# Folding 1/rms out of the two matmul units that follow each RMS norm

## The chip, the cores and the metric

The kernel runs on one core of a Trainium2 chip. The metric is the device time of one execution in microseconds (us), as the median of several runs. Everything is float32; the products are split in high and low parts ("hi" and "lo") so that three fp32r matmuls stand for one fp32 product.

## The reference

Two blocks of two layers each, sequence 512, width 1024, feed-forward width 2816. A layer of the first block has three RMS norms with a learned scale and shift ("adaLN"), a layer of the second block has two plain ones:

```python
def rms_norm(x, g):
    y = x * lax.rsqrt(jnp.mean(x * x, axis=-1, keepdims=True) + EPS)
    return y * g

def adaln_pre(h, g, shift, scale):
    return rms_norm(h, g) * (1 + scale) + shift

# first block, each of 2 layers; mod comes from (silu(c) @ ada_w[l] + ada_b[l])
h = adaln_pre(x, norm_g[l, 0], ...)
x = x + 0.5 * gate0 * swiglu(h, ffn1_w13[l], ffn1_w2[l])
h = adaln_pre(x, norm_g[l, 1], ...)
y = four mixers of (h @ w_in[l] + b_in[l])
x = x + gate1 * (y @ w_out[l])
h = adaln_pre(x, norm_g[l, 2], ...)
x = x + 0.5 * gate2 * swiglu(h, ffn2_w13[l], ffn2_w2[l])
# second block, each of 2 layers
h = h + mixers2(rmsnorm(h, attn_norm[l]) @ w_in[l]) @ w_out[l]
h = h + conv_ffn(rmsnorm(h, ffn_norm[l]), w_up[l], conv_w[l], conv_b[l], w_down[l])
# at the end
return rmsnorm(h, final_norm)
```

## The kernel before, in words

**Layout.** x is kept transposed in SBUF as `xT`, 8 tiles of 128 channels by 512 positions. A norm writes the tiles `hH[k]` (rounded to fp32r) and `hL[k]` (the rest), k from 0 to 7. A "unit" is one block of weights, 8 tiles of 128x128 (11 for the feed-forward's second matrix), which gives one 128x512 output in a PSUM bank: for each k the matmuls wH.hH, wL.hH and wH.hL, so 24 (or 33) matmuls a unit. In the whole program there are 508 units and TensorE (PE) does them in one fixed order.

**Engines.** Every engine has its own hand-written program and they meet on semaphores alone. For unit u:
- SyncE (SP) loads the weights into `wR[u % 2]` (`unit`, L926). It waits until the low part of unit u-2 is made.
- ScalarE (ACT) makes the high part `wH` (`hi`, L1021), after the load has landed and unit u-2 has been used by PE (semaphore `w_used`).
- VectorE (DVE) makes the low part `wL` (`lo`, L1476).
- PE multiplies (`products`, L2472) and DVE or ACT evicts the bank.

The third unit after a norm has buffers of its own (`third`, L1028, L1470), so that it can be made ready while the first two are still in use.

**Between two matmul stages** the order is: PE ends the last unit; DVE adds its output to x (`add_to_x`, L1517, in `down` or `project_out`); ACT squares the last tile of x (`last_square`, L1088); GpSimd (POOL) has by then squared and summed tiles 0 to 6 (`square_sum`, L2333, which takes two instructions a tile); PE sums both over the channels with two fp32 products by ones (`mean_square`, L2550); ACT takes Ln and Exp (`inverse_root`, L1096) and has `rstd`; then the norm proper (DVE `norm`, L1570, and ACT `norm`, L1070) for each k: DVE `hf` = x * modA * rstd, ACT `hH` = hf + shift, DVE `hL` = hf + shift - hH. `hf` has two buffers. PE begins the first two units with `first_two` (L2484), which for each k does both units' three matmuls as soon as `hL[k]` is there (semaphore `h_lo`).

**Adaptive weights.** While the feed-forward's up stage runs, SP also loads the columns of `ada_w` (`stream_ada`, L938). The first two pairs of them go to SBUF that the norm uses, so SP waits for the last `h_lo` of the norm first; four loads of 512 KB are issued then, and the load of the stage's fifth unit (index 4) stands behind them on SP's queue:

```python
turn(1, 1, False)                                   # units 2 and 3
sp.wait_ge(S.h_lo, at(S.h_lo, KT * (norm + 1)))     # L954
tiles(0, 0, False)
tiles(1, 1, False)
with sp.Fori(1, turns // 2) as i:                   # unit 4 and on
```

**Boundaries.** There are eleven norms: the first (at the start of the program), nine between two matmul stages, and the final one. The nine are: from the first feed-forward's down stage to the mixers (2), from the mixers' output projection to the second feed-forward's up stage (2), from that one's down stage to the next layer's up stage (1), from a down stage to the second block's mixers (2), and from the second block's output projection to its up stage with a convolution (2, `up2`, L2273, L3039). The first five have a shift, the last four have none.

**Mixers.** The mixers of both blocks are run in small steps between quarters of the units (`mixers_in`, L1897 for DVE and L2759 for PE). In the first block, the first unit's output goes on through a chain of small operations of DVE and ACT (steps "gates", "decay"), and PE needs their result at the end of the fourth unit (`d_running`).

## Time and profile before

| | |
|---|---|
| runs | 3773.61 us median of 3 (3773.47 to 3783.66) |
| the profiled execution | 3782.82 us, of which the span of the core is 3781.0 us |
| granted TensorE clock, mean | 0.955 of full speed |
| PE busy | 3545.8 us, 94% of the span |
| DVE busy | 1971.7 us, 52% |
| ACT busy | 1126.3 us, 30% |
| POOL busy | 333.9 us, 9% |
| DMA | 102 GB/s over the span |

The profiled execution is 9.2 us above the median of the runs. Shares of busy time are averages over all stages; PE's busy time is modelled from pipelined matmuls. In the timelines a row gives the start, the duration, the engine, the source line, the output and the inputs, how many instructions are merged, and in brackets how long the engine was idle before and what released it.

### The profile page before, as it was taken

What the parts mean: (1) busy time and instruction counts of PE and PEld (TensorE: products, weight loads), DVE (VectorE), ACT (ScalarE), POOL (GpSimd) and SP (SyncE); (2) the same over time, 40 slices, a digit from 0 to 9 for tenths busy, and PEclk for the clock granted to TensorE, in tenths of its full rate; (3) what the DMA queues carried; (4) which work ended last, traced back from release to release, by engine and by line L of the source; (5) the groups of instructions that cost most, each with busy time, mean ns of one, the idle gap of its engine ahead of it and who ended that gap; (6) DMA issues with size and microseconds to landing.
All of it is one profiled execution on the core that took longest, in us unless ns stands there. A gap on an engine that the chain in (4) does not pass through costs nothing. (4 is left out here: it accounts for less than half of the span.)

```text
span 3781.0 us, 45308 instructions
## 1 busy us (share of the span) xinstructions
PE 3545.8 (94%) x16234; PEld 2837.9 (75%) x16234; DVE 1971.7 (52%) x3061; ACT 1126.3 (30%) x1612; POOL 333.9 (9%) x271
## 2 busy tenths in 40 slices
PE   4999998998999999999898899999899999989998
PEld 2888766786888788877677778886678887668887
DVE  6563445553653366434555366435746633656643
ACT  1222333422222222223343132213433323333321
POOL 2000100131000100010013100010110001110001
PEclk7999999997999999999998899999999999999999
DMA  6553222101543255322210045321122232122232
GB/s 253 198 190 111 84 67 79 51 1 45 183 178 101 83 199 189 125 88 67 78 54 9 28 166 191 109 99 62 62 67 96 93 106 83 56 74 83 94 108 76
DMA packets 99362, 386.25 MB, mean 102 GB/s; under 512 B 10974, under 2 KB 12126, under 8 KB 98872
## 3 DMA queue, kind: packets, MB, share of 16 engines
q1 hardware_dynamic: 99256, 384.82, 29.3%
q8 instruction: 68, 1.11, 0.1%
q14 instruction: 38, 0.31, 0.0%
HBM read 382.65 MB, written 2.12 MB: 102 GB/s over the span
## 5 line engine op out<-in xcount | busy, mean ns | idle before, releaser
L1026 ACT ACTIVATE wH<-wR 128x1024 fp32r<-128x1024 f32 (+1 forms) x494 | 554.3, 1122 | 1834.3 <-PE bank L2481 1475.0
L1479 DVE TENSOR_TENSOR wL<-wR,wH 128x1024 fp32r<-128x1024 f32 (+1 forms) x494 | 652.6, 1321 | 793.6 <-ACT wH L1026 793.6
L2479 PE MATMUL bank<-hH,wH 128*128 128x512 f32 x2128 | 827.8, 389 | 0.0
L2480 PE MATMUL bank<-hH,wL 128*128 128x512 f32 x2128 | 827.8, 389 | 0.0
L2481 PE MATMUL bank<-hL,wH 128*128 128x512 f32 x2128 | 827.8, 389 | 0.0
L2479 PEld LDWEIGHTS bank<-hH,wH 128*128 128x128 f32 x2128 | 399.5, 188 | 83.0
L2481 PEld LDWEIGHTS bank<-hL,wH 128*128 128x128 f32 x2128 | 399.5, 188 | 82.8
L2480 PEld LDWEIGHTS bank<-hH,wL 128*128 128x128 f32 x2128 | 399.5, 188 | 82.7
L2479 PE MATMUL bank<-gH,wH 128*128 128x512 f32 x1056 | 410.8, 389 | 0.0
L2480 PE MATMUL bank<-gH,wL 128*128 128x512 f32 x1056 | 410.8, 389 | 0.0
L2481 PE MATMUL bank<-gL,wH 128*128 128x512 f32 x1056 | 410.8, 389 | 0.0
L2560 PE MATMUL bank<-hH,wH 128*128 128x512 f32 x704 | 307.3, 437 | 9.9 <-DVE wL L1479 9.9
L2562 PE MATMUL bank<-hL,wH 128*128 128x512 f32 x704 | 283.4, 403 | 0.0
L2561 PE MATMUL bank<-hH,wL 128*128 128x512 f32 x704 | 282.7, 402 | 0.0
L2481 PEld LDWEIGHTS bank<-gL,wH 128*128 128x128 f32 x1056 | 198.2, 188 | 41.2
L2480 PEld LDWEIGHTS bank<-gH,wL 128*128 128x128 f32 x1056 | 198.2, 188 | 41.1
L2479 PEld LDWEIGHTS bank<-gH,wH 128*128 128x128 f32 x1056 | 198.2, 188 | 41.0
L1497 DVE TENSOR_TENSOR gf<-bank,sil 128x512 f32<-128x512 f32 x88 | 60.9, 692 | 272.2 <-PE bank L2481 258.1
L2279 DVE SCALAR_TENSOR_TENSOR xn<-bank,par,xn 128x511 f32<-128x511 f32 (+1 forms) x176 | 131.6, 748 | 134.3 <-ACT xn L1388 122.4
L2560 PEld LDWEIGHTS bank<-hH,wH 128*128 128x128 f32 x704 | 137.6, 196 | 59.0 <-issue 21.5
L1438 DVE CUSTOM_DVE_ANT_0 adaw<-adaw,cond 128x1024 f32<-128x1024 f32 x144 | 170.3, 1221 | 0.0
L2340 POOL TENSOR_TENSOR sumsq<-xT 128x512 f32<-128x512 f32 x11 | 11.5, 1042 | 1752.8 <-DVE xT L1517 1732.9
(383 smaller groups left out, 4065.5 us busy)
## 6 DMA issues: line engine op xcount, KB each, us to landing
wR<-in_ffn_w SPq DMA_DIRECT2D x176, 512.0 KB, 3.4
adaw<-in_ada_w SPq DMA_DIRECT2D x144, 512.0 KB, 4.0
wR<-in_ffn_w SPq DMA_DIRECT2D x64, 704.0 KB, 4.0
wR<-in_w_up SPq DMA_DIRECT2D x88, 512.0 KB, 3.2
wR<-in_w_mix SPq DMA_DIRECT2D x76, 512.0 KB, 3.3
wR<-in_w_down SPq DMA_DIRECT2D x32, 704.0 KB, 4.1
wR<-in_w_in SPq DMA_DIRECT2D x40, 512.0 KB, 3.2
wR<-in_w_out SPq DMA_DIRECT2D x32, 512.0 KB, 3.2
```

The costliest lines, as they stand in the source:

```text
L1026: act.activation(wH[n][:, 0:tiles, :], wR[n][:, 0:tiles, :], ACT.Copy).then_inc(S.w_hi, 1)
L1438: return dve.tensor_tensor_reduce(w, w, cond[:, :], 1.0, 0.0, ALU.mult, ALU.add, dst)
L1479: dve.tensor_tensor(wL[n][:, 0:tiles, :], wR[n][:, 0:tiles, :], wH[n][:, 0:tiles, :].bitcast(F32), ALU.subtract).then_inc(S.w_lo, 1)
L1497: dve.tensor_tensor(gf[:, :], bank[1][:, :], sil[:, :], ALU.mult).then_inc(S.g_mul, 1)
L2279: dve.scalar_tensor_tensor(y, bank[half][:, 0:T - d], par[:, bass.ds(E_CW + 3 * (i + FT * half) + 2 - d, 1)], y, ALU.mult, ALU.add).then_i ...
L2340: pool.tensor_tensor(dst[:, :], xT[:, m, :], xT[:, m, :], ALU.mult).then_inc(S.pool, 1)
L2479: pe.matmul(o, wH[n][:, k, :], rH[:, r, :], start=start and k == 0, stop=False)
L2480: pe.matmul(o, wL[n][:, k, :], rH[:, r, :], start=False, stop=False)
L2481: mm = pe.matmul(o, wH[n][:, k, :], rL[:, r, :], start=False, stop=stop and k == tiles - 1)
L2560: pe.matmul(o, wH[n][:, k, :], hH[:, k, :], start=k == 0, stop=False)
L2561: pe.matmul(o, wL[n][:, k, :], hH[:, k, :], start=False, stop=False)
L2562: mm = pe.matmul(o, wH[n][:, k, :], hL[:, k, :], start=False, stop=k == KT - 1)
```

## The change

1. After each of the nine norms between stages, the first two units are no longer multiplied by the normalised h. ACT and DVE make, tile by tile in the stage before, the high and low parts of x * modA (`u_hi`, `u_lo`), and PE multiplies these (`pair`) into banks 4 and 5. Their eviction multiplies by `rstd`, and adds, where the norm has a shift, the constant (shift . W), which DVE sums from the raw weights in 16 instructions of 128x128 (`shift_sums`) and PE reduces with two products by one column of ones.
2. The mean square's two products move into that run, behind the matmuls of k = 1.
3. From the third unit on the products still use h. Its tiles are made in `norm` as before, but the scaled x of the odd tiles now comes from POOL, in two instructions (x * rstd, then * modA), and the third unit's matmuls wait for `h_lo` tile by tile. This holds for the norm at the start too, which keeps `first_two`.
4. So that the weights of those first two units are ready at the boundary, the last unit of the stage before gets buffers of its own (`last`, or `third`), and `hi_next` and `lo_next` make both units' parts while it runs. The table load for Ln and Exp moves to the start of the down stage.

On every engine the loops over the layers of both blocks become one, the `par` loads move ahead of the stage that they followed, and in the output projection DVE adds to x before it makes the next unit's low part. The core of the diff:

```diff
@@ DVE
+            def u_lo(to, hi, sub, ubase, k):
+
+                dve.wait_ge(S.u_hi, at(S.u_hi, ubase + k + 1))
+                dve.scalar_tensor_tensor(to[:, k, :], xT[:, k, :], modA[:, bass.ds(sub * KT + k, 1)],
+                                         hi[:, k, :].bitcast(F32), ALU.mult, ALU.subtract).then_inc(S.u_lo, 1)
+
+            def shift_sums(u, sub, n):
+
+                for b in range(2):
+                    dve.wait_ge(S.w_in[b], at(S.w_in[b], 16 * (u // 2 + 1)))
+                    o = gf[:, b * P:(b + 1) * P]
+                    for k in range(KT):
+                        m = mod[:, 3 * sub * KT + k:3 * sub * KT + k + 1]
+                        c = 2 * KT * n + KT * b + k
+                        if k:
+                            dve.wait_ge(S.shift, at(S.shift, c))
+                            dve.scalar_tensor_tensor(o, wR[b][:, k, :], m, o, ALU.mult, ALU.add).then_inc(S.shift, 1)
+                        else:
+                            dve.tensor_scalar(o, wR[b][:, k, :], m, None, ALU.mult).then_inc(S.shift, 1)
...
+            def project_out(ubase, sub, follow, base, shift=None):
+
+                for j in range(KT):
+                    dve.wait_ge(S.w_used, at(S.w_used, ubase + j + 1))
+                    add_to_x(j, j % 2, sub)
+                    if 1 <= j < KT - 3:
+                        lo(ubase + j + 2, KT, j % 2)
+                    elif j == KT - 3:
+                        lo_last(ubase + KT - 1, third, KT)
+                    elif j == KT - 2:
+                        if shift is not None:
+                            shift_sums(ubase + KT, follow, shift)
+                        lo_next(ubase + KT)
+                    u_lo(uL, uH, follow, base, j)
...
                 for k in range(KT):
-                    if k >= 2:
-                        dve.wait_ge(S.h_lo, at(S.h_lo, KT * n + k - 1))
-                    dve.scalar_tensor_tensor(hf[:, k % 2, :], xT[:, k, :], modA[:, sub * KT + k:sub * KT + k + 1], rstd[:, :],
-                                             ALU.mult, ALU.mult).then_inc(S.hf, 1)
+                    if k % 2 == 0:
+                        if k:
+                            dve.wait_ge(S.h_lo, at(S.h_lo, KT * n + k - 1))
+                        dve.scalar_tensor_tensor(hf[:, 0, :], xT[:, k, :], modA[:, sub * KT + k:sub * KT + k + 1], rstd[:, :],
+                                                 ALU.mult, ALU.mult).then_inc(S.hf, 1)
                     if k:
                         low(k - 1)
...
+                if not start:
+                    lo(u + 3, KT, 1)
                 low(KT - 1)
@@ POOL
+            def norm(n, sub, first=False):
...
+                pool.wait_ge(S.rstd, at(S.rstd, n + 1))
+                for k in range(1, KT, 2):
+                    if k > 1:
+                        pool.wait_ge(S.h_lo, at(S.h_lo, KT * n + k - 1))
+                    pool.tensor_tensor(hf[:, 1, :], xT[:, k, :], rstd[:, :], ALU.mult).then_inc(S.hf_x, 1)
+                    pool.wait_ge(S.hf_x, at(S.hf_x, KT // 2 * n + k // 2 + 1))
+                    pool.tensor_scalar(hf[:, 1, :], hf[:, 1, :], modA[:, sub * KT + k:sub * KT + k + 1], None,
+                                       ALU.mult).then_inc(S.hf_p, 1)
@@ PE
+            def pair(u, moving, n, ubase, shifts=None):
+
+                xH, xL = moving
+                pe.wait_ge(S.w_lo, at(S.w_lo, u + 2))
                 for k in range(KT):
+                    pe.wait_ge(S.u_lo, at(S.u_lo, ubase + k + 1))
+                    for b in range(2):
+                        o = bank[4 + b][:, :]
+                        pe.matmul(o, wH[b][:, k, :], xH[:, k, :], start=k == 0, stop=False)
+                        pe.matmul(o, wL[b][:, k, :], xH[:, k, :], start=False, stop=False)
+                        mm = pe.matmul(o, wH[b][:, k, :], xL[:, k, :], start=False, stop=k == KT - 1)
...
+                    if k == 1:
+                        if shifts is not None:
+                            pe.wait_ge(S.shift, at(S.shift, 2 * KT * (shifts + 1)))
+                            for b in range(2):
+                                mm = pe.matmul(bank[7][:, b:b + 1], gf[:, b * P:(b + 1) * P], ones[:, 0:1], start=True, stop=True)
+                            mm.then_inc(S.shift_ps, 1)
+                        mean_square(n)
+
+            def products_third(o, ready=None):
+
+                for k in range(KT):
+                    if ready is not None:
+                        pe.wait_ge(S.h_lo, at(S.h_lo, ready + k + 1))
                     pe.matmul(o, third[0][:, k, :], hH[:, k, :], start=k == 0, stop=False)
@@ ACT
+            def hi_next(u):
+
+                hi(u, u // 2 + 1, KT, 0)
+                hi(u + 1, u // 2 + 1, KT, 1, behind=3)
+
+            def u_hi(to, sub, xbase, k):
+
+                act.wait_ge(S.x_new, at(S.x_new, xbase + k + 1))
+                act.activation(to[:, k, :], xT[:, k, :], ACT.Identity,
+                               scale=modA[:, bass.ds(sub * KT + k, 1)]).then_inc(S.u_hi, 1)
@@ DVE, up: the pair's eviction, after norm
+                    if pair is not None and not later(i):
+                        dve.wait_ge(S.shift_ps, at(S.shift_ps, shifts + 1))
+                        dve.tensor_copy(cc[:, :], bank[7][:, 0:2]).then_inc(S.pair, 1)
+                        dve.wait_ge(S.w_used, at(S.w_used, ubase + 2))
+                        dve.tensor_tensor(sil[:, :], bank[4][:, :], rstd[:, :], ALU.mult).then_inc(S.pair, 1)
+                        dve.tensor_tensor(gf[:, :], bank[5][:, :], rstd[:, :], ALU.mult).then_inc(S.pair, 1)
+                        dve.wait_ge(S.pair, at(S.pair, pair + 3))
+                        dve.wait_ge(S.sil, at(S.sil, gbase + 1))
+                        dve.scalar_tensor_tensor(gf[:, :], gf[:, :], cc[:, 1:2], sil[:, :], ALU.add, ALU.mult).then_inc(S.g_mul, 1)
```

## Rows read from the trace of the kernel before

**Rows 1.** The waits of PE: engine, tile, line, releaser, us in total, times, longest.

```profile
PE bank L2490 <- DVE hL L1574: 34.7, 9, 3.9
PE bank L2555 <- ACT sqt L1092: 25.8, 10, 3.4
```

**Rows 2.** Windows around one boundary: us, busy by engine (count), clock, DMA share, GB/s.

```profile
937.20:946.90 9.70, 3.21 (x5) 0.80 (x5) 5.43 (x8) 6.62 (x8) 0.19 (x1) 0.65 0.16 54
946.90:950.40 3.50, 3.47 (x8) 2.82 (x9) 3.43 (x6) 1.45 (x2) 0.00 (x0) 0.50 0.00 0
950.40:970.80 20.40, 20.30 (x89) 16.44 (x88) 12.36 (x19) 7.39 (x9) 0.00 (x0) 1.00 0.61 218
```

**Rows 3.** Timeline of that boundary, from the output projection to the up stage.

```profile
936.82 0.39 PE L2481 MATMUL bank<-hL,wH 128*128 128x512 f32 x1
...
939.53 0.75 DVE L1517 SCALAR_TENSOR_TENSOR xT<-bank,gate,xT 128x512 f32<-128x512 f32 x1
...
943.11 0.69 ACT L1098 ACTIVATE rstd<-bank,cst 128x512 f32<-128x512 f32 x1 [1.22 <-PE bank L2555]
...
944.49 1.41 DVE L1582 SCALAR_TENSOR_TENSOR hf<-xT,modA,rstd 128x512 f32<-128x512 f32 x2 [1.28 <-ACT rstd L1101]
...
946.93 0.77 PE L2490 MATMUL bank<-hH,wH 128*128 128x512 f32 x1 [3.86 <-DVE hL L1574]
...
954.74 1.63 DVE L1574 SCALAR_TENSOR_TENSOR hL<-hf,mod,hH 128x512 fp32r<-128x512 f32 x2
...
970.82 0.39 PE L2479 MATMUL bank<-hH,wH 128*128 128x512 f32 x1
```

**Rows 4.** The same boundary: SP's queue, and ACT waiting for the fifth unit's load.

```profile
956.39 1.75 SPq L946 DMA_DIRECT2D adaw<-in_ada_w  x4
...
965.72 1.06 ACT L1026 ACTIVATE wH<-wR 128x1024 fp32r<-128x1024 f32 x1 [4.85 <-DMA wR<-in_ffn_w]
...
ACT wH L1026 <- DMA wR<-in_ffn_w: 15.6, 3, 5.4
```

**Rows 5.** Groups by line and shape: busy us, mean ns of one, idle before.

```profile
L2343 POOL TENSOR_TENSOR sumsq<-sumsq,rstd 128x512 f32<-128x512 f32 x66 | 85.5, 1295 | 5.2
...
L2340 POOL TENSOR_TENSOR sumsq<-xT 128x512 f32<-128x512 f32 x11 | 11.5, 1042 | 1752.8 <-DVE xT L1517 1732.9 <-DVE xT L1435 19.9
...
L1574 DVE SCALAR_TENSOR_TENSOR hL<-hf,mod,hH 128x512 fp32r<-128x512 f32 x80 | 59.8, 748 | 2.6
...
L1479 DVE TENSOR_TENSOR wL<-wR,wH 128x1024 fp32r<-128x1024 f32 x398 | 496.5, 1248 | 332.0 <-ACT wH L1026 332.0
...
L2167 DVE SCALAR_TENSOR_TENSOR AD<-LG,RT 128x128 f32<-128x128 f32 x8 | 2.8, 353 | 0.3
...
L1080 ACT ACTIVATE hH<-hf,mod 128x512 fp32r<-128x512 f32 x80 | 57.3, 724 | 70.3 <-DVE hf L1582 70.3
```

**Rows 6.** Timeline where POOL and DVE both read SBUF.

```profile
543.36 1.04 POOL L2356 TENSOR_TENSOR hf<-pm 128x512 f32<-128x512 f32 x1 [82.13 <-DVE pm L1902]
...
543.68 1.80 DVE L1479 TENSOR_TENSOR wL<-wR,wH 128x1024 fp32r<-128x1024 f32 x1 [0.40 <-ACT wH L1026]
...
26.27 10.78 POOL L2340 TENSOR_TENSOR rstd<-xT 128x512 f32<-128x512 f32 x1
```

**Rows 7.** Timeline of PE: an fp32 product between fp32r matmuls at full clock.

```profile
557.51 1.02 PE L2589 MATMUL bank<-hf,cst 128*128 128x512 f32 x2
...
558.60 0.40 PE L2561 MATMUL bank<-hH,wL 128*128 128x512 f32 x1
```

**Rows 8.** Timeline of PE: unit 4 after the boundaries to mixers and to up2.

```profile
437.69 0.39 PE L2481 MATMUL bank<-gL,wH 128*128 128x512 f32 x1
...
474.13 0.50 PE L2560 MATMUL bank<-hH,wH 128*128 128x512 f32 x1
...
2786.93 0.39 PE L2481 MATMUL bank<-hL,wH 128*128 128x512 f32 x1
...
2822.66 0.39 PE L2479 MATMUL bank<-hH,wH 128*128 128x512 f32 x1
```

More of the change, by code:

```diff
@@ L32 @@
 L = 2
+N_LAYERS = 2 * L
 FF = 2816
@@ L755, in build @@
         S.h_lo = sem("h_lo")
+        S.hf_x = sem("hf_x")
+        S.hf_p = sem("hf_p")
+        S.u_hi = sem("u_hi")
+        S.u_lo = sem("u_lo")
+        S.u_used = sem("u_used")
+        S.shift = sem("shift")
+        S.shift_ps = sem("shift_ps")
+        S.pair = sem("pair")
         S.mixc_in0 = sem("mixc_in0")
@@ L1518, in add_to_x, with down, tile @@
                                          xT[:, m, :], ALU.mult, ALU.add).then_inc(S.x_new, 1)
[L1520 to L1527 removed]
+            def down(ubase, sub, follow, base, between=None, shift=None):
+                def tile(m, b):
+                    for n in range(2):
+                        lo(ubase + 2 * m + 2 + n, KH, n)
                     dve.wait_ge(S.w_used, at(S.w_used, ubase + 2 * m + 2))
                     add_to_x(m, b, sub)
+                    if follow is not None:
+                        u_lo(hL, hH, follow, base, m)
                 for j in range(2 if between else 0):
                     for n in range(2):
[L1532 removed]
+                        tile(2 * j + n, 2 + n)
                         between(2 * j + n)
@@ L1570, in norm @@
-            def norm(n, sub, u=2, start=False):
+                        tile(2 * j + n, 2 + n)
+                u = ubase + 2 * KT
+                lo(u - 2, KH, 0)
+                lo_last(u - 1, last, KH)
+                dve.wait_ge(S.w_used, at(S.w_used, u - 2))
+                add_to_x(KT - 2, 2, sub)
+                if follow is not None:
+                    u_lo(hL, hH, follow, base, KT - 2)
+                    if shift is not None:
+                        shift_sums(u, follow, shift)
+                    lo_next(u)
@@ L1572, in low, with norm @@
+            def norm(n, sub, u, start=False):
                 def low(k):
@@ L1588, in norm @@
                             lo(b, KT, b)
+                if not start:
+                    lo(u + 3, KT, 1)
                 low(KT - 1)
@@ L2411, in layer1 @@
                 square_sum(KT, 2)
-            for l in range(L):
-                begin(l)
-                layer1(l)
+                norm(2, 2)
             def y_square(h):
@@ L2439, in layer2 @@
                 square_sum(0, 1)
-            for l in range(L):
-                begin(L + l)
-                layer2(l)
+                norm(1, 1)
+            for l in range(N_LAYERS):
+                begin(l)
+                if l < L:
+                    layer1(l)
+                else:
+                    layer2(l - L)
             begin(2 * L)
@@ L2512, in turn @@
                     pe.wait_ge(S.w_lo, at(S.w_lo, ubase + 2 * i + 2))
-                    pe.wait_ge(S.g_mul, at(S.g_mul, gbase + i))
+                    if not tiles or not third:
+                        pe.wait_ge(S.g_mul, at(S.g_mul, gbase + i))
                     products(bank[1][:, :], 1, KT, hH, hL, 0, True, True)
-                first_two(ubase, ready)
+                if tiles:
+                    pair(ubase, tiles, n, xbase, shifts)
+                else:
+                    mean_square(n)
+                    first_two(ubase, (S.h_lo, KT * n))
                 turn(1, True)
```

507 lines of the change are left out of this document (291 added, 216 removed).

## The prediction

> **What bounds the kernel now.** First the table: PE is busy for 94% of the span, so the time is the length of PE's queue plus its waits, and anything that makes PE wait longer at a boundary is added one for one. Second, PE's waits: between the stages it waits for the norm's tiles (9 waits, up to 3.9 us) and for the last tile's square (10, up to 3.4), 60.5 us in all [rows 1]. Third, one boundary of the mixers-to-up kind. Its last matmul ends at 936.82 + 0.39 = 937.21, which I call T0; the sum for x comes at 939.53, rstd begins at 943.11, the norm at 944.49, and PE's first product of the up stage at 946.93, 9.7 us after T0 [rows 3]. The windows add the clock: in those 9.7 us PE does 3.21 us of work, then it runs 8 matmuls in 3.5 us at a granted 0.50 (1.2 GHz), 0.43 us each, then 89 in 20.4 us, 0.229 each, at 1.00 (2.4 GHz) [rows 2]. The cold start costs 8 x 0.20 = 1.7 us. The prize is the idle 6.5 us plus this 1.7, at nine boundaries: about 70 us, if PE found work until h is ready and h came no later.
>
> My measure for every boundary is the start of the fifth unit (index 4), because units 0 to 3 are the ones that change. It is T0 + 33.6 here (970.82) [rows 3], T0 + 36.05 before the mixers and T0 + 35.3 before up2 [rows 8]. Two things precede it: the end of h, called H (954.74 + 1.63 = 956.37, so 11.9 after the norm began) [rows 3], and a load. SP waits for the last h_lo, issues four ada_w loads at 956.39, and only then unit 4's load, which ACT gets at 965.72; with the high part (1.06) and the low part (1.25) [rows 4, 5] and its handoffs unit 4 can't start before H + 11.8. ACT waits for that load 15.6 us in three stages already [rows 4].
>
> **Removed: the wait before the pair.** PE goes into x * modA at once. rstd is then found inside: 12 matmuls of 0.229 = 2.75, the shift's two products, and two fp32 products. One of these took 558.60 - 557.51 - 0.23 = 0.86 [rows 7]. The shift's products have one column and no row here; an estimate from four weight loads is 0.8 (bounds: 0 and, as full products, 1.7). 2.75 + 0.8 + 1.72 + 0.05 = 5.3, plus 1.4 from the product's end to the norm's start (943.11 to 944.49 is 1.38) [rows 3]: the norm starts at R = T0 + 6.7, or 5.9 where there is no shift. Before it was 7.3. The norm starts hardly earlier, and PE has 11 us of pair and then needs h tile by tile.
>
> **Moved: hf of the odd tiles, to POOL.** This decides the sum. POOL's two-input operation on 128x512 takes 1.295 us; for the second one, with one input and a scalar, the nearest row is the square at 1.042 [rows 5]. I take 1.04; bounds 0.52 (half of it) and 1.295. A round makes two tiles, and each round's POOL work waits for the h_lo of the last one's odd tile, since POOL has one buffer, so it is a closed loop: POOL 1.29 + 1.04, ACT's hH 0.72, DVE's hL 0.75 [rows 5], and 0.35 of handoffs (0.08 on POOL, 0.14, 0.10, 0.03) = 4.15. The DVE pipeline of before made two tiles in 11.9 / 4 = 3.0. On top comes contention. While POOL had an operation of 1.04 at 543.36, DVE's low part, started at 543.68, took 1.80 in place of 1.25 [rows 6, 5]; and a POOL square of 1.04 took 10.78 with DVE at work on weights [rows 6]. Both read SBUF; so do hf, hL and lo, each with two SBUF inputs, in every round. I put 0.9 a round on it (bounds 0 and 2). That makes 5.1, 5.0, 5.0, and 5.5 for the last, where lo(u + 3) with its 1.25 goes ahead of the last hL: 20.5 in place of 11.9. H = T0 + 27.2 with a shift, 26.4 without (before 19.2). The third unit ends 0.85 after H and PE waits in it.
> The Trainium skill (GPSIMD Engine Reference, Elementwise — side-by-side cycle accounting) gives a one-input operation of 512 elements about 0.77 us; by it the round would be 0.27 shorter and the forecast would be 3815. No row here shows that form.
>
> **Boundary by boundary, unit 4 after T0.** A unit takes 24 x 0.229 = 5.5 us.
> - Down to ada up (1): H + 11.8 for the load, PE is out of work after the fourth unit and gets cold again (1.7): 27.2 + 11.8 + 1.7 = 40.7, against 33.6: +7.1.
> - Mixers to ada up (2): here the shift sums do harm. DVE gets to them after the sum for tile 6, at T0 - 4.7, and they are 16 x 0.383 = 6.1 (0.353 [rows 5] and 0.03 between dependent ones), with POOL's squares in the way +1.6; the two low parts (2.46) and u_lo of tile 6 (0.75) come behind them, and PE's pair waits on `w_lo`. It starts at -4.7 + 6.1 + 1.6 + 2.5 + 0.7 = T0 + 6.2. Then the norm starts at 6.7 + 6.2 + 1.7 (cold) = 14.6, H = 35.1, and unit 4 = 35.1 + 11.8 + 1.7 = 48.6: +15.0 each, +30.0. Queued behind the sums on DVE are also the last sum for x and its low part, but these are ready at 8, before PE's 12 matmuls end.
> - Down to the first block's mixers (2): after H, DVE evicts the pair and does the first unit's chain, which PE needs at the end of the fourth unit: some twelve operations of 0.75 with handoffs of 0.13, 10.6 (estimate). 37.8 against 36.05: +1.8 each, +3.6. PE's own work would allow 27.2 + 0.85 + 5.5 + 1.7 = 35.3.
> - Down to the second block's mixers (2): no shift, PE's own work sets it: 26.4 + 0.85 + 5.5 + 1.7 = 34.4, and before about as the first (33.6, not shown): +0.8 each, +1.6.
> - Projection to up2 (2): pair's eviction and convolution behind the norm on DVE, some 8, then unit 4's low part 1.25 and 1.0 of handoffs: 26.4 + 10.3 + 1.7 = 38.4 against 35.3: +3.1 each, +6.2.
> - The start's norm gets the split alone, no pair: H 20.5 - 11.9 = up to 8.6 later; PE had about half of that in hand: +4.
> Hidden, at nothing: `u_hi` and `u_lo` (0.72 and 0.75 eight times a boundary [rows 5]), which lie in the stage before, where the windows give ACT and DVE room (DVE 52%, ACT 30% of the span); the same windows' share would price them at their sum, 12 us a boundary, if that cover were gone. Merged loops and moved `par` loads: nothing, one small load issued earlier on SP ahead of loads that wait anyway; at worst one issue a stage (956.39's four took 1.75, 0.44 each [rows 4]), 2 to 3 us in all.
>
> **Sum:** 7.1 + 30.0 + 3.6 + 1.6 + 6.2 + 4 = 52.5. The profiled execution, 3782.8, would become about 3835; it lies 9.2 above the median, so the median goes from 3773.6 to 3826, rounded 3825. Ten norms of four rounds stand in it, so each 0.1 on a round is worth 4 us: the total is 52.5 - 40 x (5.1 - round), and zero at a round of 3.8.
>
> **Rivals.**
> - *Faster (7%).* The other side by one mechanism: POOL's second operation takes 0.52 and never meets DVE at the port. The round is 3.6 to 3.7 and, with shift sums that cost little, H comes early enough that PE runs from T0 to unit 4 almost without a stop: 3751. It decides at a round of 3.8. For it: the 66 operations of 1.295 [rows 5] run while DVE works on weights and their mean isn't much stretched. Against it: the 1.80 [rows 6].
> - *No change (11%).* No contention, but POOL at 1.04: rounds 4.15, less 40 x 0.95 = 38, and with the shift sums as forecast, some 12 us better than that remainder because the last lo is then also free of stalls: 3776.
> - *The shift sums are covered (15%).* If the weights of the pair are there earlier and the sums start a unit sooner, or run faster than 0.383, the pair starts at T0 + 0: the mixers-to-up boundary falls by up to 9 each, 18 in all: 3808.
> - *Worse (12%).* DVE's operations follow each other without a gap and starve POOL, as in the 10.78 [rows 6], and the clock falls to 1.2 GHz inside the third unit: 1.5 more at each of ten norms, 3840.
> - That the change doesn't do what it says (PE still waits for rstd) isn't likely: the pair's operands have no rstd in them; I give it nothing of its own.
> The forecast keeps 55%.
>
> **Numbers.** A measurement of this kernel can tell about 0.3%, 11.3 us, from no change. 3825; the range goes from 3786 (shift sums covered and POOL's second operation at 0.52, which alone takes 40 x 0.52 = 21 off) to 3845 (1.295 for it, +10, and cold clock). Outside are the first two rivals and little else. Faster 0.07, same 0.11, slower 0.82.
>
> **What would show it.** In the profile of after: PE's wait for hL moves from the pair to the third unit, `products_third`, four or more waits a boundary of 3 to 4 us; POOL's two operations in `norm` at 1.3 and 1.0 or stretched beyond, DVE's hL and hf beside them over 0.75; from the norm's start to the last hL 20 us instead of 11.9; PE's wait for `w_lo` before the pair after the mixers, about 6 us, twice; ACT's wait for the ada_w-delayed load longer than 5.4; the clock at 0.50 inside the third unit. Wrong would be: a round under 4.0 us, no PE wait in the third unit, or a pair that starts late at other boundaries than the two.

## The result, and the profile after

The change makes the kernel slower: 3827.62 us as the median of 4 runs (3821.71 to 3836.13), against 3777.19 for the kernel before in the same comparison (4 runs, 3773.47 to 3783.66). The ratio is 1.0133, with a 95% interval of 1.0105 to 1.0161. The forecast was 3825. The profiled execution of after has a span of 3829.9 us, 48.9 more than the one before.

The head of the page of after, with the busy time and share of each engine:

```profile
PE 3561.2 (93%) x16254; PEld 2848.8 (74%) x16254; DVE 2107.1 (55%) x3192; ACT 1167.3 (30%) x1682; POOL 509.1 (13%) x351
```

PE is busy 15 us longer than before, though it runs only 20 matmuls more (16254 against 16234, the added ones with a single column): most of it is matmuls at the lower clock, since the mean granted clock is 0.952 against 0.955. Some 33 of the 48.9 us are waits of PE. DVE and POOL have gained 135 and 175 us, none of it at an engine's limit. So the shares tell little, and the waits of PE come next (us in total, times, longest):

```profile
PE bank L2693 <- DVE hL L1698: 40.6, 15, 3.9
PE bank L2771 <- DVE hL L1698: 30.9, 12, 3.7
...
PE bank L2673 <- DVE wL L1596: 10.5, 2, 5.2
...
PE bank L2639 <- DVE wL L1596: 8.3, 3, 3.8
```

The two waits of before [rows 1], 34.7 for the norm's tiles in the first two units and 25.8 for the last square, are gone between the stages. In their place PE waits 40.6 + 30.9 us for hL in the third unit (L2693 in the up stages, L2771 in the mixers), 27 times and up to 3.9 us each; 10.5 for the low parts of the pair's weights, twice 5.2; and 8.3 for the fifth unit's.

The boundary of [rows 3, 4] again, from the mixers' projection to the up stage. T0 is 941.57 now. First DVE ahead of the pair (timeline: start, duration, engine, line, output and inputs):

```profile
936.17 0.75 DVE L1645 SCALAR_TENSOR_TENSOR xT<-bank,gate,xT 128x512 f32<-128x512 f32 x1 [2.11 <-PE bank L2641]
...
937.15 4.42 DVE L1589 SCALAR_TENSOR_TENSOR gf<-wR,mod,gf 128x128 f32<-128x128 f32 x7
...
941.79 2.68 DVE L1589 SCALAR_TENSOR_TENSOR gf<-wR,mod,gf 128x128 f32<-128x128 f32 x7
944.39 2.35 DVE L1596 TENSOR_TENSOR wL<-wR,wH 128x1024 fp32r<-128x1024 f32 x2
```
```profile
946.80 0.79 PE L2673 MATMUL bank<-uH,wH 128*128 128x512 f32 x1 [5.23 <-DVE wL L1596]
```

The sum for tile 6 ends at 936.9; the shift sums fill DVE until 944.5, the two low parts until 946.7, and only then may PE start, 5.2 after T0. Seven of the 128x128 instructions took 4.42 the first time and 2.68 the second: in the first stretch POOL squared and summed tile 6 of x beside them (937.06 to 939.47).

Then the norm, on POOL, ACT and DVE:

```profile
955.61 1.29 POOL L2497 TENSOR_TENSOR hf<-xT,rstd 128x512 f32<-128x512 f32 x1 [16.13 <-ACT rstd L1187]
957.00 1.89 POOL L2499 TENSOR_SCALAR hf<-hf,modA 128x512 f32<-128x512 f32 x1
960.52 1.29 POOL L2497 TENSOR_TENSOR hf<-xT,rstd 128x512 f32<-128x512 f32 x1 [1.64 <-DVE hL L1698]
961.91 1.88 POOL L2499 TENSOR_SCALAR hf<-hf,modA 128x512 f32<-128x512 f32 x1
965.42 1.73 POOL L2497 TENSOR_TENSOR hf<-xT,rstd 128x512 f32<-128x512 f32 x1 [1.62 <-DVE hL L1698]
967.25 1.88 POOL L2499 TENSOR_SCALAR hf<-hf,modA 128x512 f32<-128x512 f32 x1
970.75 1.72 POOL L2497 TENSOR_TENSOR hf<-xT,rstd 128x512 f32<-128x512 f32 x1 [1.62 <-DVE hL L1698]
972.58 2.42 POOL L2499 TENSOR_SCALAR hf<-hf,modA 128x512 f32<-128x512 f32 x1
```
```profile
958.92 0.72 ACT L1170 ACTIVATE hH<-hf,mod 128x512 fp32r<-128x512 f32 x1 [0.71 <-POOL hf L2499]
```
```profile
955.57 1.88 DVE L1707 SCALAR_TENSOR_TENSOR hf<-xT,modA,rstd 128x512 f32<-128x512 f32 x1 [4.02 <-ACT rstd L1187]
...
959.69 2.67 DVE L1698 SCALAR_TENSOR_TENSOR hL<-hf,mod,hH 128x512 fp32r<-128x512 f32 x2
...
975.78 0.75 DVE L1698 SCALAR_TENSOR_TENSOR hL<-hf,mod,hH 128x512 fp32r<-128x512 f32 x1 [2.22 <-ACT hH L1170]
```

A round reads: POOL x * rstd 955.61 to 956.90, * modA 957.00 to 958.89, ACT 958.92 to 959.64, DVE's hL from 959.69 (the first of its row) to about 960.4, and POOL's next at 960.52. That is 4.91. From one start of x * rstd to the next the rounds are 4.91, 4.90 and 5.33, and the last, to H, is 5.8, with the low part lo(u + 3) of DVE beside it and POOL's * modA at 2.42. H is 976.53, 20.9 after the norm's start, where it was 11.9 [rows 3]. The other eight boundaries show the same rounds to within 0.3. POOL's * modA takes 1.88 at best here, and DVE's first hf took 1.88 in place of 0.75; it began 0.04 before POOL's x * rstd and ran beside it.

By group, mean ns of one and what came before (busy us, mean ns | idle before); the first two are POOL's, the others DVE's:

```profile
L2499 POOL TENSOR_SCALAR hf<-hf,modA 128x512 f32<-128x512 f32 x40 | 81.4, 2035 | 3.9
...
L2497 POOL TENSOR_TENSOR hf<-xT,rstd 128x512 f32<-128x512 f32 x40 | 60.2, 1505 | 205.8 <-ACT rstd L1187 134.3 <-DVE hL L1698 48.9 <-DVE gate L2179 22.7
```
```profile
L1698 DVE SCALAR_TENSOR_TENSOR hL<-hf,mod,hH 128x512 fp32r<-128x512 f32 x80 | 68.5, 877 | 65.3 <-ACT hH L1170 64.2
...
L1707 DVE SCALAR_TENSOR_TENSOR hf<-xT,modA,rstd 128x512 f32<-128x512 f32 x40 | 53.2, 1331 | 21.2 <-ACT rstd L1187 20.1
...
L1576 DVE SCALAR_TENSOR_TENSOR uL<-xT,modA,uH 128x512 fp32r<-128x512 f32 x32 | 43.0, 1342 | 6.3 <-ACT uH L1079 6.3
```

POOL's * modA has a mean of 2035 ns, x * rstd of 1505. hL was 748 ns in [rows 5] and is 877; hf was 751 in the trace of before and is 1331; the new low part uL, which I had at 0.75, takes 1342 where it meets POOL's squares.

Last, windows of the same boundary (busy us by engine and count, granted clock, DMA share, GB/s): the pair until the norm begins, the norm, and until the fifth unit runs:

```profile
946.80:955.60 8.80, 8.80 (x27) 6.47 (x28) 3.28 (x5) 3.51 (x5) 0.00 (x0) 0.73 0.32 113
955.60:976.50 20.90, 12.39 (x51) 8.96 (x49) 14.15 (x14) 7.25 (x10) 14.10 (x8) 0.89 0.00 1
976.50:990.20 13.70, 11.26 (x35) 8.71 (x36) 9.36 (x17) 3.76 (x5) 0.00 (x0) 0.75 0.86 331
...
972.00:982.00 10.00, 6.07 (x15) 4.25 (x14) 7.36 (x11) 2.73 (x3) 2.89 (x2) 0.50 0.43 158
```

In the norm's 20.9 us PE is busy 12.4. The clock is 0.73 in the first window and 0.75 in the third. These are means of 1.00 and 0.50 (1.2 GHz). The last window shows a stretch at 0.50, which begins amid the third unit's waits and lasts until 982; another goes from 989 to 992, just after unit 4 has begun. Each time PE had waited before.

SP's queue and ACT at the end:

```profile
976.56 1.76 SPq L983 DMA_DIRECT2D adaw<-in_ada_w  x4
```
```profile
985.49 1.06 ACT L1064 ACTIVATE wH<-wR 128x1024 fp32r<-128x1024 f32 x1 [7.53 <-DMA wR<-in_ffn_w]
```

The load of the fifth unit stands behind ada_w as in [rows 4]; ACT gets it 9 us after H again and waits 7.53 for it, and this time PE has nothing left: unit 4 starts at 987.94, T0 + 46.4.

I took T0 of each boundary and H from both timelines. The column "growth" is what the interval from this T0 to the next grew by in the profiled executions, which is the boundary's cost plus whatever else changed in the stage:

| boundary | H before | H after | forecast H | growth | forecast |
|---|---|---|---|---|---|
| start | - | - | - | +1.4 | +4 |
| down to mixers, 1st layer | 19.2 | 27.3 | 27.2 | +3.0 | +1.8 |
| mixers to up, 1st | 19.2 | 35.0 | 35.1 | +14.5 | +15.0 |
| down to up | 19.7 | 27.3 | 27.2 | +7.2 | +7.1 |
| down to mixers, 2nd layer | 18.8 | 27.3 | 27.2 | -0.9 | +1.8 |
| mixers to up, 2nd | 19.2 | 34.9 | 35.1 | +14.2 | +15.0 |
| down to second block's mixers (2) | 19.4, 18.4 | 27.1, 27.1 | 26.4 | -2.5, +1.5 | +0.8 each |
| projection to up2 (2) | 19.2, 18.2 | 27.0, 27.0 | 26.4 | +4.2, +6.2 | +3.1 each |
| final norm | | | | +0.3 | 0 |
| sum (of unrounded growths) | | | | +48.9 | +52.5 |

H is counted from T0. The growth over the stages of the mixers isn't a clean measure of the boundary: it moved by several us between kernels that don't differ there (see the last section). The forecast's own measure, the start of unit 4 after T0, is cleaner there. The same trace gives it:

| boundary | unit 4 before | unit 4 after | forecast |
|---|---|---|---|
| down to mixers, both layers | 36.1, 36.1 | 38.9, 38.9 | 37.8 |
| mixers to up, both layers | 33.6, 33.8 | 46.4, 46.2 | 48.6 |
| down to up | 34.4 | 39.0 | 40.7 |
| down to second block's mixers (2) | 34.9, 33.4 | 36.2, 36.1 | 34.4 |
| projection to up2 (2) | 35.3, 34.3 | 37.8, 37.8 | 38.4 |

The growths of unit 4 add up to 45.4 us, and the start adds 1.4.

### The profile page after: what moved, and what is told of

Same layout as the page of the kernel before. It is cut to its first block, busy times and chain, and to the rows that moved or that the text cites. A ratio compares the mean times of both kernels' runs of the same rounds, so it can differ in the third digit from the quotient of the medians.

```text
span 3829.9 us, 45620 instructions
## 1 busy us (share of the span) xinstructions
PE 3561.2 (93%) x16254; PEld 2848.8 (74%) x16254; DVE 2107.1 (55%) x3192; ACT 1167.3 (30%) x1682; POOL 509.1 (13%) x351
## 4 chain that ended last, share of the span: by engine, by line
PE 82%; DVE 8%; ACT 4%; POOL 3%; issue 2%; DMA 1%; SPq 0%; DVEq 0%; ACTq 0%
PE bank L2639 18%; PE bank L2641 18%; PE bank L2640 18%; PE bank L2761 4%; PE bank L2763 4%; PE bank L2762 4%; POOL hf L2499 2%; POOL hf L2497 1%; PE bank L3047 1%; PE bank L2861 1%; PE bank L3057 1%; PE bank L3043 1%; DVE hL L1698 1%; ACT wH L1064 1%; DVE wL L1596 1%
## 5 line engine op out<-in xcount | busy, mean ns | idle before, releaser
L1064 ACT ACTIVATE wH<-wR 128x1024 fp32r<-128x1024 f32 (+1 forms) x484 | 539.8, 1117 | 1539.4 <-PE bank L2641 1262.8
L2639 PE MATMUL bank<-hH,wH 128*128 128x512 f32 x2096 | 823.1, 393 | 12.4 <-DVE wL L1596 8.3
L2639 PE MATMUL bank<-gH,wH 128*128 128x512 f32 x990 | 385.1, 389 | 0.0
L2640 PE MATMUL bank<-gH,wL 128*128 128x512 f32 x990 | 385.1, 389 | 0.0
L2641 PE MATMUL bank<-gL,wH 128*128 128x512 f32 x990 | 385.1, 389 | 0.0
L2482 POOL TENSOR_TENSOR sumsq<-xT 128x512 f32<-128x512 f32 x11 | 11.5, 1042 | 1603.5 <-DVE xT L1645 1584.9
L2640 PEld LDWEIGHTS bank<-gH,wL 128*128 128x128 f32 x990 | 185.8, 188 | 38.7
L2639 PEld LDWEIGHTS bank<-gH,wH 128*128 128x128 f32 x990 | 185.8, 188 | 38.5
L2641 PEld LDWEIGHTS bank<-gL,wH 128*128 128x128 f32 x990 | 185.8, 188 | 38.5
```

Of the source, the lines that this page charges most:

```text
L1064: act.activation(wH[n][:, 0:tiles, :], wR[n][:, 0:tiles, :], ACT.Copy).then_inc(S.w_hi, 1)
L2639: pe.matmul(o, wH[n][:, k, :], rH[:, r, :], start=start and k == 0, stop=False)
L2640: pe.matmul(o, wL[n][:, k, :], rH[:, r, :], start=False, stop=False)
L2641: mm = pe.matmul(o, wH[n][:, k, :], rL[:, r, :], start=False, stop=stop and k == tiles - 1)
```

## The experiments

The kernel before ran beside every group of experiments: its median was 3774.96 us (17 runs) beside experiments 1 to 4, 3779.96 (7) beside 5 to 8 and 3775.86 (15) beside 9. So times of different groups can't be compared to better than about 5 us, and the ratio of each is to the kernel before of its own group. Each experiment begins with its median in us.

**1. POOL out of the norm.**

```diff
@@ DVE norm
-                    if k % 2 == 0:
-                        if k:
-                            dve.wait_ge(S.h_lo, at(S.h_lo, KT * n + k - 1))
-                        dve.scalar_tensor_tensor(hf[:, 0, :], xT[:, k, :], modA[:, sub * KT + k:sub * KT + k + 1], rstd[:, :],
-                                                 ALU.mult, ALU.mult).then_inc(S.hf, 1)
+                    if k >= 2:
+                        dve.wait_ge(S.h_lo, at(S.h_lo, KT * n + k - 1))
+                    dve.scalar_tensor_tensor(hf[:, k % 2, :], xT[:, k, :], modA[:, sub * KT + k:sub * KT + k + 1], rstd[:, :],
+                                             ALU.mult, ALU.mult).then_inc(S.hf_p if k % 2 else S.hf, 1)
@@ POOL norm
-                pool.wait_ge(S.rstd, at(S.rstd, n + 1))
-                for k in range(1, KT, 2):
...
+                pass
```

> The change with one part undone: DVE makes the scaled x of the odd tiles as well, with one instruction each and the wait on h_lo of two tiles earlier, as before the change; POOL does nothing in the norm. Theory A (the norm's rounds of two tiles, 5.2 us each with POOL in them, set the end of h and so the start of the fifth unit): from the norm's start to the last hL 12 us instead of 20.9, PE's waits for hL in the third unit nearly gone, and the whole kernel at 3750 (about 78 below the changed kernel and 27 below the one before: -5 at each mixers boundary, -6 and -5 at those of the second block, -4 at down-to-up, +4 at each output-projection-to-up, where the pair still starts 5 late). Rival B (the loss sits in the late start of the pair, the shift sums and the loads; POOL's rounds are only where PE happens to wait): at most 15 us come back, 3813 or more.

3751.72 (ratio 0.9936 to before, 0.9924 to 0.9948). With one part undone a loss of 50 becomes a gain of 23. The waits of PE and DVE's groups:

```profile
PE bank L2629 <- DVE wL L1596: 15.2, 3, 5.4
...
PE bank L2663 <- DVE wL L1596: 10.5, 2, 5.2
...
PE bank L2683 <- DVE hL L1698: 5.1, 10, 0.8
PE bank L2761 <- DVE hL L1698: 4.1, 8, 0.8
```
```profile
L1698 DVE SCALAR_TENSOR_TENSOR hL<-hf,mod,hH 128x512 fp32r<-128x512 f32 x80 | 59.8, 747 | 1.4
L1706 DVE SCALAR_TENSOR_TENSOR hf<-xT,modA,rstd 128x512 f32<-128x512 f32 x80 | 59.3, 751 | 21.9 <-ACT rstd L1187 19.8
```

The waits for hL fell from 71.5 to 9.2 us. hL and hf are back at 747 and 751 ns, and h ends 12.8 after the norm's start. That is H = T0 + 19.1 behind a down stage with a shift, 18.7 to 18.9 without one, and 26.8 and 26.5 at the two boundaries from mixers to up, where the pair still starts late (2 x 5.2). The wait for the fifth unit's load is also left and is now longer: 15.2 in three waits instead of 8.3. Theory A held, boundary by boundary too: against the kernel before, unit 4 starts 5.4 earlier after both first-block mixers boundaries (expected 5), 8.7 and 7.3 after the second block's, 3.9 at down-to-up (4), 5.4 and 4.6 at up2, and 4.5 and 4.7 later at mixers to up (4).

Not all of the 76 us that come back against the changed kernel are waits. In the traces, whose spans differ by 78.1, PE's busy time falls from 3561.2 to 3532.7 with the same 16254 matmuls, and the mean clock rises from 0.952 to 0.963: so some 28 us are matmuls that no longer run at the low clock (as far as PE's modelled busy time can tell).

**2. Half of the shift sums one tile earlier.**

```diff
 elif j == KT - 2:
     if shift is not None:
-        shift_sums(ubase + KT, follow, shift)
+        shift_sums(ubase + KT, follow, shift, (1,))
     lo_next(ubase + KT)
 u_lo(uL, uH, follow, base, j)
+if j == KT - 3 and shift is not None:
+    shift_sums(ubase + KT, follow, shift, (0,))
```

> The change with the shift sums of the first of the two units made one output tile earlier in the output projection; the second's stay where they are. Only the two boundaries from the mixers' projection to the up stage have room to change. Theory A (PE's wait for w_lo before the pair, 5.2 us, is 16 instructions of 0.35 to 0.6 us on DVE that run too late): the wait falls to about 1.5, the norm and everything after it comes 3.7 earlier, 7.5 us in all, 3820. Rival B (the weights of the pair, not the sums, are late, or the sums just push the sum for x of tile 6 back): the wait stays above 4.5 and the time at 3827.

3825.39 (ratio 1.0132, 1.0118 to 1.0147). In time this can't be told from the changed kernel (1.0133). In the trace the wait fell by 1.2 at each of the two boundaries, to 4.05, less than theory A had and more than rival B. The two intervals shrank by 2.2 each. DVE's timeline shows rival B's second mechanism at work:

```profile
932.60 1.53 DVE L1576 SCALAR_TENSOR_TENSOR uL<-xT,modA,uH 128x512 fp32r<-128x512 f32 x1
934.05 1.31 DVE L1591 TENSOR_SCALAR gf<-wR,mod 128x128 f32<-128x128 f32 x1
935.39 2.68 DVE L1589 SCALAR_TENSOR_TENSOR gf<-wR,mod,gf 128x128 f32<-128x128 f32 x7
937.98 0.74 DVE L1645 SCALAR_TENSOR_TENSOR xT<-bank,gate,xT 128x512 f32<-128x512 f32 x1
...
938.96 4.41 DVE L1589 SCALAR_TENSOR_TENSOR gf<-wR,mod,gf 128x128 f32<-128x128 f32 x7
```

The first eight sums took from 934.05 to 938.0, with 1.31 for the first one, beside a POOL operation that ran until 935.27. So the sum for tile 6 slipped from 936.17 to 937.98. DVE had 2.1 us free there, not 4, and the u_lo ahead of the sums had itself taken 1.53. POOL's squares of tile 6 slipped too, and stretched the second eight as they had stretched the first eight before (4.41 for seven). DVE is full in the last two tiles of the projection, so this order saved little.

**3. The fifth unit's load before ada_w.**

```diff
 turn(1, 1, False)
+unit(ubase + 4, w[l, 4], KT, 0)
 sp.wait_ge(S.h_lo, at(S.h_lo, KT * (norm + 1)))
 tiles(0, 0, False)
 tiles(1, 1, False)
-with sp.Fori(1, turns // 2) as i:
+unit(ubase + 5, w[l, 5], KT, 1)
+tiles(2, 0)
+turn(3, 1, True)
+with sp.Fori(2, turns // 2) as i:
```

> The change with SP's order altered in the up stage: the load of unit 4 is issued before SP waits for the last h_lo and the four loads of ada_w; unit 5 behind them. Theory A (after the rounds, the fifth unit waits for its load, 11.4 us after H, at the three adaLN up boundaries): unit 4 starts when PE has done units 2 and 3, 8 us after H; 3.5 us come back at each of three, about 11 in all with some of the cold clock, 3816. Rival B (the wait just moves to unit 5, whose load is now behind ada_w): 3 us or less come back, 3825.

3814.51 (ratio 1.0097, 1.0083 to 1.0112), 13 below the changed kernel, or 11 if each is taken from the kernel before of its own group. In the trace the three intervals fell from +14.5, +7.2, +14.2 to +10.3, +0.8, +10.2 against before; PE's wait for hL stayed at 41.1 and that of unit 4 for its low part is gone. Theory A held; ACT still waits 18.6 us for such loads, at later units, where PE doesn't run dry.

**4. POOL's second operation left out.** The odd tiles of h miss modA.

```diff
-    pool.tensor_tensor(hf[:, 1, :], xT[:, k, :], rstd[:, :], ALU.mult).then_inc(S.hf_x, 1)
-    pool.wait_ge(S.hf_x, at(S.hf_x, KT // 2 * n + k // 2 + 1))
-    pool.tensor_scalar(hf[:, 1, :], hf[:, 1, :], modA[:, sub * KT + k:sub * KT + k + 1], None,
-                       ALU.mult).then_inc(S.hf_p, 1)
+    pool.tensor_tensor(hf[:, 1, :], xT[:, k, :], rstd[:, :], ALU.mult).then_inc(S.hf_p, 1)
```

> The change with POOL's second operation left out: the odd tiles of h miss the factor modA, POOL does x * rstd alone. Theory A (the second operation, 1.9 us in the trace against the 1.04 forecast, is the largest term of the round): a round falls from 5.2 to about 3.3, norm's start to last hL 13, and the time to about 3760. Rival B (the port between POOL and DVE is what costs, whatever POOL does): rounds stay above 4.2 and the time above 3790.

3769.25 (ratio 0.9983, 0.9974 to 0.9992). The norm takes 15.3 us to the last hL (behind a down stage with a shift, the norm's start R is T0 + 6.3 and H is T0 + 21.6), so a round is 3.8 on average, and 58 of the 76 us that experiment 1 gave back hang on this one operation. The average hides two things: the middle rounds are 3.37, as theory A had (3.3), and the first stays at 4.91 although half of POOL's work is gone from it. The rows are the first round of the boundary from mixers to up, then POOL's and DVE's groups:

```profile
942.07 1.29 POOL L2497 TENSOR_TENSOR hf<-xT,rstd 128x512 f32<-128x512 f32 x1 [15.92 <-ACT rstd L1187]
946.98 1.29 POOL L2497 TENSOR_TENSOR hf<-xT,rstd 128x512 f32<-128x512 f32 x1 [3.62 <-DVE hL L1698]
```
```profile
942.02 1.88 DVE L1707 SCALAR_TENSOR_TENSOR hf<-xT,modA,rstd 128x512 f32<-128x512 f32 x1 [3.81 <-ACT rstd L1187]
```
```profile
L2497 POOL TENSOR_TENSOR hf<-xT,rstd 128x512 f32<-128x512 f32 x40 | 51.5, 1289 | 236.7 <-ACT rstd L1187 134.0 <-DVE hL L1698 80.0 <-DVE gate L2179 22.7
```
```profile
L1698 DVE SCALAR_TENSOR_TENSOR hL<-hf,mod,hH 128x512 fp32r<-128x512 f32 x80 | 89.8, 1123 | 11.9 <-ACT hH L1170 8.2
...
L1707 DVE SCALAR_TENSOR_TENSOR hf<-xT,modA,rstd 128x512 f32<-128x512 f32 x40 | 41.3, 1033 | 21.0 <-ACT rstd L1187 19.9
```

POOL's operation is undisturbed (1289 ns), but hL now takes 1123 and hf 1033 in the mean. In the first round it is DVE that decides: its first hf takes 1.88 beside POOL instead of 0.75, and hL[0], the next hf and hL[1] follow one another behind it. In the middle rounds an hL beside POOL takes 1.9 and pushes the hL that POOL waits for back by some 0.5. So the meeting of POOL and DVE is a real second term, which rival B had; it isn't the main one.

**5. POOL's operations by themselves.** In the first 13 us of the program both engines are free.

```diff
@@ POOL
+            pool.tensor_scalar(sil[:, :], gf[:, :], gf[:, 0:1], None, ALU.mult).then_inc(S.bench, 1)
+            pool.wait_ge(S.bench, 3)
+            pool.tensor_scalar(sil[:, :], gf[:, :], 1.5, None, ALU.mult).then_inc(S.bench, 1)
...
+            pool.wait_ge(S.bench, 5)
+            pool.tensor_tensor(sil[:, :], gf[:, :], sqt[:, :], ALU.mult).then_inc(S.bench, 1)
...
@@ DVE
+            dve.wait_ge(S.bench, 6)
+            for r in range(6):
+                if r:
+                    dve.wait_ge(S.bench_v, r)
+                dve.scalar_tensor_tensor(rstd[:, :], gf[:, :], gf[:, 0:1], sqt[:, :], ALU.mult, ALU.mult).then_inc(S.bench_v, 1)
```

> The changed kernel with a row of POOL operations on 128x512 put ahead of it, in the first 13 us in which POOL and DVE have nothing else: first with DVE idle a tensor_scalar with a scalar from SBUF, one with a constant, one from SBUF again, a tensor_tensor; then tensor_tensor and two tensor_scalar beside six scalar_tensor_tensor of DVE that read two SBUF tiles. Theory A (POOL's operation with one input and a scalar is slow by itself): 1.57 alone (the shortest of the trace), tensor_tensor 1.29, and up to 1.9 or more beside DVE. Rival B (it takes the 1.04 of the forecast when alone and was stretched to 1.9 by DVE): 1.04 with DVE idle and 1.6 to 1.9 beside it.

```profile
1.81 1.57 POOL L2484 TENSOR_SCALAR sil<-gf 128x512 f32<-128x512 f32 x1
3.46 1.49 POOL L2486 TENSOR_SCALAR sil<-gf 128x512 f32<-128x512 f32 x1
...
6.69 1.26 POOL L2490 TENSOR_TENSOR sil<-gf,sqt 128x512 f32<-128x512 f32 x1
8.03 1.26 POOL L2492 TENSOR_TENSOR sil<-gf,sqt 128x512 f32<-128x512 f32 x1
9.39 1.88 POOL L2494 TENSOR_SCALAR sil<-gf 128x512 f32<-128x512 f32 x1
11.37 1.79 POOL L2496 TENSOR_SCALAR sil<-gf 128x512 f32<-128x512 f32 x1
```
```profile
7.99 6.41 DVE L1524 SCALAR_TENSOR_TENSOR rstd<-gf,sqt 128x512 f32<-128x512 f32 x6 [7.14 <-POOL sil L2490]
```

This kernel ran once (3839.3 us), and only its trace is used. Alone the tensor_scalar takes 1.57 (1.49 with a constant), more than the two-input tensor_tensor with 1.26. Beside DVE it takes 1.88 and 1.79. DVE's six took 6.41 us against 6 x 0.75 = 4.5. So the length is the operation's own, +0.53 on what I had, and 0.2 to 0.3 of waiting come on top. Theory A held.

The Trainium skill (GPSIMD Engine Reference, Elementwise — side-by-side cycle accounting) gives 0.77 us as the best case for 512 elements; this form takes twice that here. The Trainium skill (SBUF — State Buffer, Who interferes with whom) states that a DVE instruction with two SBUF inputs contends with a GpSimd instruction that reads SBUF. The trace agrees: 6.41 against 4.5 for DVE, and 1.88 against 1.57 for POOL.

**6. All three edits together.**

> The three edits together: odd tiles on DVE, the first unit's shift sums one tile earlier, and the load of unit 4 ahead of ada_w. Theory A (the rounds, the pair's late start and the load are separate terms on PE's path): 3751.7 less some 12 for the load and 2 for the sums, 3738, which is 37 under the kernel before. Rival B (with h 9 us earlier, the load or the sums no longer decide): 3749 to 3752.

3739.43 (ratio 0.9890, 0.9874 to 0.9907): as expected, and 1.1% under the kernel before. This is the version to keep. The two added edits bring 12.3 us on experiment 1 in plain times, and 17 if each is taken from the kernel before of its own group (-23.2 and -40.5); 14 were expected. So the terms add up as far as this can tell.

**7. Without most of the shift sums.** Experiments 1 and 3 together, and of the sums only the first of eight tiles is computed.

```diff
-    if k:
-        dve.wait_ge(S.shift, at(S.shift, c))
-        dve.scalar_tensor_tensor(o, wR[b][:, k, :], m, o, ALU.mult, ALU.add).then_inc(S.shift, 1)
-    else:
-        dve.tensor_scalar(o, wR[b][:, k, :], m, None, ALU.mult).then_inc(S.shift, 1)
+    if k == 0:
+        dve.tensor_scalar(o, wR[b][:, k, :], m, None, ALU.mult).then_inc(S.shift, KT)
```

> Odd tiles on DVE and the load of unit 4 first, and of the shift sums only the first of eight tiles is computed (the rest of shift . W is left out), so that DVE does 2 instructions in place of 16. Theory A (the sums delay the pair by 5.2 us at the two boundaries after the mixers' projection and nowhere else): 10 us under the same kernel with its sums, 3729. Rival B (the wait there is for the pair's weights or low parts): 3738 or more.

3719.96 (ratio 0.9844, 0.9824 to 0.9863), 19.5 below experiment 6. The pair starts at T0 + 0.0 at both boundaries, so theory A's place is right; its price was too small. Against experiment 6 the intervals of those two boundaries fell by 6.6 and 6.3, of which 4.05 is the wait and 2.4 to 2.7 the low clock behind it: the norm begins 9.3 and 9.0 after the pair's start with the wait, 6.6 without it. The remaining 6 or so of the 19.5 lie in the mixers' stages and weren't separated from the clock's changes there.

**8. The split alone, on the kernel before.** POOL's function, its semaphores and the halved loop of DVE as in the change, nothing else.

```diff
@@ DVE norm
-                    if k >= 2:
-                        dve.wait_ge(S.h_lo, at(S.h_lo, KT * n + k - 1))
...
+                    if k % 2 == 0:
+                        if k:
+                            dve.wait_ge(S.h_lo, at(S.h_lo, KT * n + k - 1))
...
@@ POOL, after square_sum
+                norm(0, 0, 3)
                 square_sum(0, 1)
+                norm(1, 1, 5)
...
```

> The kernel before with one part of the change alone: POOL makes the scaled x of the odd tiles in its two operations; no pair, no shift sums. Theory A (the split alone costs 8.7 us at each of ten norms, and all of it lies on PE's path, since PE then waits tile by tile from the start): 3775 + 75 to 87, 3850 to 3862. Rival B (some of it is hidden behind the loads of the fifth unit and the mixers' chains): 3810 to 3835.

3848.96 (ratio 1.0180, 1.0163 to 1.0197), 69 more than the kernel before of its group.

```profile
PE bank L2513 <- DVE hL L1579: 80.4, 37, 4.0
```

PE waits 80.4 us for hL in 37 waits instead of 34.7 in 9 [rows 1]. H moved from 18.2 to 19.7 after T0 to between 27.4 and 28.9. The time is at the lower end of theory A, but the growth of 69 is 6 less than its 75, since the kernel before ran 5 slower in this group than it had assumed: a part is hidden, as rival B had. The profiled execution is by 19 us the fastest of its five, 46 above the one of before; in it the mixers ran at a higher clock (see the last section). The starts of unit 4 are free of that: they moved by 6.2 to 8.8 at the nine boundaries, 65.6 in all, and the first interval grew by 3.8, together 69.4. With experiment 1 this gives the change as a sum: the pair and its belongings are worth -23, the split +69 to +76.

**9. The load edit on the kernel before.** The diff of experiment 3.

> The kernel before with the load edit alone: unit 4's load is issued ahead of SP's wait for the last h_lo and of the ada_w loads. Theory A (before the change this wait was 15.6 us in three stages, and it is a flaw of both kernels): some 10 to 13 us come back, 3765, so that of the combined version's gain of 37 about a third is the load's and the rest the pair's. Rival B (the loads that get behind it, unit 5's and ada_w's, take the wait over where h is early): under 4 us, and the pair has the whole gain.

3777.65 (ratio 1.0007, 0.9993 to 1.0020), which is no change, where I had expected 10. In its trace ACT waits for no such load any more, and the time is still the same. In [rows 2] PE is busy 20.30 of the 20.40 us up to unit 4, so ACT's wait in [rows 4] was covered before the change. The load costs only where PE has run out of work, so no part of the 40 us of experiment 6 could be had by this edit without the pair.

## Why the prediction was right

- **PE's queue plus its waits.** This held in the main, but the queue's own length moves with the clock: from the changed kernel to experiment 1, some 50 of 78 us are waits and some 28 are matmuls at the low clock. The forecast had 1.7 for each restart and nothing else.
- **The wait before the pair is removed, the norm starts hardly earlier.** This held. R is 6.3 with a shift (forecast 6.7) and 5.9 to 6.1 without (5.9). The two waits of [rows 1] are gone.
- **POOL's split decides the sum, round 5.1, H - R 20.5.** This held in total, with 20.9, and experiments 1 and 8 show it: 76 us come back when it goes, 69 are lost when it comes alone. Its terms were mis-sized in opposite senses. I took 1.04 for "the second operation", the nearest row's value, and bounded it by 0.52 and 1.295; it takes 1.57 alone (experiment 5), outside those bounds. I took 0.9 for contention and 0.35 for handoffs; the mean round of 5.2 less 1.29, 1.57, 0.72, 0.75 and 0.26 of handoffs (0.10, 0.03, 0.05, 0.08) leaves 0.6. The errors, +0.53 on the operation and -0.4 on contention and handoffs, nearly cancel. The total rested on luck by that much: with contention at 0.9 and the right length the forecast would have been 20 higher, at the upper end of the range. The four terms of the rounds also add up to 20.6, not 20.5.
- **The total is linear in the round, zero at 3.8.** This is nearly so: experiment 4 has a mean round of 3.8 and measures 0.9983 of before.
- **The shift sums start the pair 6.2 late.** It starts 5.2 late, both times. The sums' stretch by POOL's squares was there (4.42 for seven, against 2.68). The interval grew by 14.5 and 14.2 (15.0). The norm begins 8.8 after the pair's start, against 6.6 in experiment 7 where the pair has no wait: 2.2 for the cold clock, and 2.4 to 2.7 in experiment 6, where I took 1.7.
- **The fifth unit waits for its load.** This held for the three adaLN up stages: unit 4 comes 11.3 to 11.8 after H (forecast 11.8), and experiment 3 took some 11 to 13 us away. The start of unit 4 itself was forecast 1.7 to 2.4 too late (48.6 and 40.7, against 46.4, 46.2 and 39.0), because the sum put the last 1.7 of cold clock ahead of unit 4. It lies behind its start (0.50 from 989 to 992), so the intervals came out as forecast.
- **The hidden parts.** u_hi and u_lo are hidden in the down stages, as said: PE waits for neither. In the projection u_lo isn't at 0.75 but at 1.34 in the mean, which experiment 2 shows to matter: it is part of what makes DVE full there.
- **Mixers, second block, up2.** The forecast was 1.8, 1.8, 0.8, 0.8, 3.1 and 3.1; the intervals grew by 3.0, -0.9, -2.5, 1.5, 4.2 and 6.2. The sums, 11.4 and 11.5, agree by luck. By the starts of unit 4 the costs are 2.8, 2.8, 1.3, 2.7, 2.4 and 3.6, some 15.5 in all: each mixers boundary was taken 0.5 to 1.9 too cheap. The chain of twelve operations behind the 1.8 was an estimate, and no experiment isolates it.
- **The start.** The interval grew by 1.4 instead of 4. The first norm starts 2.5 sooner in that execution (67.2 against 69.7 us), and h ends 4.0 later; in experiment 8, where it starts at 69.6, the growth is 3.8. Its start varies from 66.9 to 69.7 between the executions, and what decides that is open.
- **The rivals.** "Faster" and "no change" didn't come. Of "worse" the clock did come: it stands at 0.50 in the third unit (972 to 982), as the list of signs had it too, but in the adaLN up stages PE has to wait for the load behind it anyway. The rival on covered sums had the price right at its two boundaries: 2.2 each by experiment 2 and 6.6 and 6.3 by experiment 7 make 17.3 (an estimate, as the two were measured in different kernels), where it had 18. The other 6 us of experiment 7's 19.5 lie elsewhere.

## What to carry to other kernels

Moving part of a balanced two-engine pipeline to a third engine is judged by the closed loop it makes (here POOL, ACT, DVE, back to POOL through one buffer), not by the load it takes off: 5.2 us for two tiles replaced 3.0. Price an operation on POOL in its exact form before it goes on the critical path: its one-input form with a scalar was the slowest of those measured here, slower than the form with two inputs. A round's mean can hide a different limit in its first turn (4.91 with or without POOL's second operation). A wait of PE costs more than its length, since matmuls at the low clock follow it. A wait that is covered today (the load behind ada_w) becomes a cost when the engine that covers it runs dry, and an edit that fixes it is worth nothing until then.
